# One order of wide and narrow matmuls in every unfolded unit, and eight wide matmuls that stream their columns in turn

## What is computed

```python
# first block
xn = rms_norm(x, norm_mix_g)
proj = xn @ w_in                       # 4 branches: LRU, pooling, short convolution, attention; and gates
merged = sum_k sigmoid(gate_k) * (y_k @ w_branch[k])
x = x + merged @ w_out
x = x + square(relu(rms_norm(x) @ w_mlp_up)) @ w_mlp_down        # 2048 -> 8192 -> 2048
# second block
u = rmsnorm(h, g_mix_pre)
proj = u @ w_in_2                      # dilated attention, stick-breaking attention, two gates
mix = (gate_a * (ya @ w_branch_a) + gate_b * (yb @ w_branch_b)) @ w_out_2
h = h + rmsnorm(mix, g_mix_post)
...                                    # w_up (2048 -> 2 x 5632), convolution, gelu gate, w_down,
...                                    # then a gate from w_ple_gate (2048 x 2048) on p @ w_ple_in
```

## Time and profile before

| | |
|---|---|
| time, median of 3 runs | 2932.04 us (2931.88 to 2932.59) |
| profiled execution: span from first to last instruction | 2929.8 us |
| TensorE matmul (PE) busy | 2918.4 us, 100% of the span |
| TensorE weight load (PEld) busy | 2570.8 us, 88% |
| VectorE (DVE), ScalarE (ACT), GpSimd (POOL) busy | 1920.8, 1510.8, 226.9 us |
| read from HBM | 542.25 MB, 186 GB/s over the span |
| granted TensorE clock | 1.000 |

### The profile page before, as it was taken

The page is one execution under the profiler, slowest core; times in us unless marked ns, Lnnn a source line. Parts: engine busy times, 40 slices in busy tenths (PEclk is TensorE's granted clock), DMA queues, the critical chain, the costliest instruction groups (busy, mean ns, idle before and its releaser), DMA issues. The chain is left out here.

```text
span 2929.8 us, 48840 instructions
## 1 busy us (share of the span) xinstructions
PE 2918.4 (100%) x17292; PEld 2570.8 (88%) x17292; DVE 1920.8 (66%) x2209; ACT 1510.8 (52%) x1896; POOL 226.9 (8%) x191
## 2 busy tenths in 40 slices
PE   9999999999999999999999999999999999999999
PEld 7888898998888888888888888988888888888888
DVE  6696765566665656656656566655787567757775
ACT  5576644455544444444544446555665455545564
POOL 1010020102101010000200000001000000010021
PEclk9999999999999999999999999999999999999999
DMA  8666667666565666656565555556565666666555
GB/s 248 165 186 180 173 183 229 184 177 191 194 192 182 195 191 187 193 181 197 180 197 180 167 161 168 185 185 208 159 201 180 199 187 187 192 187 187 186 158 173
DMA packets 543861, 545.94 MB, mean 186 GB/s; under 512 B 17304, under 2 KB 542112, under 8 KB 543744
## 3 DMA queue, kind: packets, MB, share of 16 engines
q1 hardware_dynamic: 540576, 536.79, 59.6%
q0 software_dynamic: 2480, 7.10, 0.9%
q10 hardware_dynamic: 688, 0.53, 0.1%
HBM read 542.25 MB, written 2.11 MB: 186 GB/s over the span
## 5 line engine op out<-in xcount | busy, mean ns | idle before, releaser
L1652 DVE TENSOR_TENSOR w_low<-raw,w_high 128x1024 fp32r<-128x1024 f32 x1012 | 1260.2, 1258 | 780.4 <-ACT w_high L1085 775.5
L1085 ACT CAST w_high<-raw 128x1024 fp32r<-128x1024 f32 x1012 | 1049.6, 1048 | 994.1 <-PE ps_gemm L704 968.9
L699 PE MATMUL ps_gemm<-act_a,w_high 128*128 128x512 f32 x4448 | 1433.5, 395 | 3.9 <-DVE act_a L2196 1.8
L699 PE MATMUL ps_gemm<-act_b,w_high 128*128 128x512 f32 x3208 | 1044.3, 395 | 0.0
L704 PEld LDWEIGHTS ps_gemm<-act_a,w_low 128*128 128x128 f32 x4608 | 861.7, 188 | 152.0
L704 PE MATMUL ps_gemm<-act_a,w_low 128*128 128x256 f32 x4608 | 991.7, 278 | 0.0
L704 PE MATMUL ps_gemm<-act_b,w_low 128*128 128x256 f32 x3520 | 778.8, 279 | 0.0
L699 PEld LDWEIGHTS ps_gemm<-act_a,w_high 128*128 128x128 f32 x4448 | 713.0, 188 | 50.4 <-issue 5.7
L704 PEld LDWEIGHTS ps_gemm<-act_b,w_low 128*128 128x128 f32 x3520 | 652.5, 189 | 96.9
L699 PEld LDWEIGHTS ps_gemm<-act_b,w_high 128*128 128x128 f32 x3208 | 524.4, 188 | 42.4
L1722 DVE TENSOR_TENSOR summ<-ps_gemm,bcopy 128x512 f32<-128x512 f32 x220 | 150.6, 685 | 8.8 <-ACT bcopy L1100 8.8
(11 more groups left out here) (291 smaller groups left out, 1204.5 us busy)
## 6 DMA issues: line engine op xcount, KB each, us to landing
raw<-in_w_in SPq DMA_DIRECT2D x348, 512.0 KB, 4.2
raw<-in_w_up SPq DMA_DIRECT2D x176, 512.0 KB, 3.5
raw<-in_w_mlp_up SPq DMA_DIRECT2D x128, 512.0 KB, 4.0
raw<-in_w_mlp_down SPq DMA_DIRECT2D x128, 512.0 KB, 3.5
raw<-in_w_down SPq DMA_DIRECT2D x88, 512.0 KB, 3.6
raw<-in_w_out SPq DMA_DIRECT2D x64, 512.0 KB, 4.7
raw<-in_w_branch SPq DMA_DIRECT2D x32, 512.0 KB, 4.0
raw<-in_w_ple_gate SPq DMA_DIRECT2D x32, 512.0 KB, 3.5
```

What stands on the lines that cost most here:

```text
L699: nc.tensor.matmul(ps[:, g, t, :], wh[:, at, o:o + P], x, start=first, stop=False, skip_group_check=True)
L1085: nc.scalar.copy(wh[:, at, :], raw[:, at, :]).then_inc(high_ready, 1)
L1652: nc.vector.tensor_tensor(wl[:, at, :], raw[:, at, :], wh[:, at, :].bitcast(F32), ALU.subtract).then_inc(split_done, 1)
```

## The change

In every unfolded unit the order within a step becomes wide, narrow, wide, narrow; folded units get the order that unfolded ones had. A table names eight phases. In these the first body is written out apart from the loop, and the very first wide matmul of the phase (first piece, k = 0, t = 0) reads and writes its 512 columns in another order: 2 (or 4) columns of the high half, the same columns of the low half, the next 2 (or 4) of the high half, and so on. Input and output follow the same order, so each column goes where it went before. There is one such matmul in each of the eight phases.

```diff
+IN_TURN = {"proj_a": 2, "gates_a2": 2, "gates_a3": 4, "gates_b1": 4, "w_out2": 2, "ffn_down0": 4, "ffn_up1": 2,
+           "ple_gate": 2}
...
-            def piece(ph, x_in, need, i, j, s, need_tile=None):
+            def piece(ph, x_in, need, i, j, s, need_tile=None, in_turn=0):
...
+                        elif k == t == 0 and in_turn:
+                            r = in_turn
+                            nc.tensor.matmul(ps[:, g, t, :].rearrange("p (e c r) -> p c e r", e=2, r=r),
+                                             wh[:, at, o:o + P], x.rearrange("p (e c r) -> p c e r", e=2, r=r),
+                                             start=first, stop=False, skip_group_check=True)
                         else:
                             nc.tensor.matmul(ps[:, g, t, :], wh[:, at, o:o + P], x,
                                              start=first, stop=False, skip_group_check=True)
...
-                    if not ph.name.startswith("mlp_"):
+                    if folded(ph, j):
                         high_product(0)
                         high_product(1)
                         low_product(0)
...
-                            piece(ph, x_in, need, i, j, s, need_tile if peeled and j == 0 else None)
+                            piece(ph, x_in, need, i, j, s, need_tile if peeled and j == 0 else None,
+                                  IN_TURN.get(ph.name, 0) if peeled and j == s == 0 else 0)
                             if once and peeled and (j, s) == at:
                                 once()
-                if once:
+                apart = once or ph.name in IN_TURN
+                if apart:
                     body(0)
-                over(pe, body, 1 if once else 0, ph.bodies)
+                over(pe, body, 1 if apart else 0, ph.bodies)
```

## The result

| | before | changed |
|---|---|---|
| time, median | 2933.43 us (7 runs, 2931.88 to 2933.58) | 2942.08 us (7 runs; six at 2937.17 to 2945.17, one at 12830.73) |
| span of the profiled execution | 2929.8 us | 2939.6 us |

The run of 12830.73 us is left out of the comparison; the other six have a median of 2941.92 us. The ratio is 1.003, 95% interval 1.002 to 1.004: about 8.5 us slower, where 7.6 us less were forecast, and outside the range. The six runs of the changed kernel are 8 us apart, those of before 2 us.

The account below looks back on a forecast made before the run. TensorE was taken to bound the kernel, by its number of matmuls times the distance between starts. Terms of -9.35 - 0.2 + 1.9 + 0 = -7.6 us took 2932.04 us to 2924.5 us, range 2922.0 to 2932.5 us.

Parts of the forecast that it names:

- What bounds the kernel: TensorE is busy 100% of the span at 2.4 GHz; time is its number of matmuls times the distance between starts.
- The order's term: Outside the mlp_ phases, all 2804 steps go from 0.69667 to 0.69333 us: -9.35 us.
- The phases that run through units. I take them quick: Phases running through units take the quick rhythm, started by eight pattern matmuls or inherited; no slow steps added there.
- called itself wrong from 280 on: Sign of failure: more than 280 of the 2804 steps slow, or a wait for `w_low` on TensorE.
- Between the small matmuls: In the two written-out stretches, a fifth of 720 steps turn slow at TensorE's restarts: +1.9 us, bounds 0 to +9.5.
- mlp_up0's start: First four pieces of mlp_up0, 16 steps, turn quick if w_out hands over the quick rhythm: -0.2 us.
- The matmuls in turn: The eight matmuls streaming columns in turn cost as much as ordinary wide ones: 0, at most 1.6 us.
- Bodies written out and buffers: Seven more phases with separate bodies on TensorE, and buffers and banks with no wait added or removed: 0.
- The order does not do it: Rival: the quick rhythm belongs to something else in the mlp_ phases, others stay as they are: 2932 us; chance 0.04.
- The rule that the prediction set beside it: Gap of N / 2.4 + 2.5 ns by columns alone: 650 ns a step in either order, the change worth nothing.
- the slow rhythm rules: Rival: slow rhythm persists after mix_* and from ffn_up0 to ffn_down2: 2947.2 us at two thirds slow, 2959.7 all; chance 0.12.

Follow-up runs that it names:

- experiment 4: Kernel before, with the order wide, wide, narrow, narrow in the mlp_ phases too and nothing of the change: 2935.62 us, ratio 1.0011.
- experiments 16 and 17: New order in chosen stretches, old-order steps as starts: first, varied counts (2944.46 us); second, one behind folded units, two behind ffn_up0's sum of squares (2927.22 us, ratio 0.998).
- experiment 16: Starts of two, three, four and one old-order steps at gates_a2, gates_a3, w_out and gates_b1, no matmul in turn: 2944.46 us, ratio 1.0042 to the kernel before.
- experiment 3: Changed kernel with the old order outside the mlp_ phases, keeping the matmuls in turn and bodies written out: 2933.29 us, ratio 1.0002.
- experiment 1: Changed kernel with an empty table: new order alone, no matmul in turn, no extra body: 2941.8 us, ratio 1.0047, runs on two levels.
- experiments 5 and 6: Changed kernel with runs of 2 in all eight phases (2938.22 us); with its table replaced by runs of 2 and 4 in mlp_ and ffn_ phases (2950.79 us).
- experiment 10: Changed kernel with single old-order steps replacing matmuls in turn, behind folded units, sums of squares and groups of small matmuls: 2929.09 us, ratio 0.9997.

## Why the prediction was wrong

- **What bounds the kernel** was right: TensorE full, no new wait, clock 1.000, the time is the distance of the starts.
- **The order's term** was right for each step (experiment 4; 88.75 against 89.17 us where it is quick) and wrong in its reach. It was taken for all 2804 steps, less a fifth of those between small matmuls.
- **"The phases that run through units. I take them quick"** is the step that failed. Its grounds were that a matmul of another pattern is a disturbance, and that the one disturbance in the trace had ended the slow rhythm. That was one case, read as a rule. A run of 4 left the slow rhythm in place (gates_a3, gates_b1, ffn_down0), a run of 2 turns the rhythm over in most states, and w_out, which had no such matmul, took the slow rhythm from the folded unit ahead of it. The prediction's own held the evidence against it: an entry into the slow rhythm with nothing irregular about it. What decides is how the last matmuls ahead stand to each other (experiments 16 and 17), and behind a folded unit they stand for slow. The changed kernel has 365 x 4 = 1460 slow steps, where the prediction called itself wrong from 280 on.
- **Sums of squares.** mlp_up0's ended the slow rhythm here as before, though not in experiment 16; slots0's and ffn_up0's started it here, for 1.2 us and 2.0 us, with ffn_down0 behind them. This was no term of the sum.
- **Between the small matmuls** a fifth was taken as slow, +1.9 us. 111 of 180 pieces were. Against the old order the two stretches lost 3.07 us, where the forecast's sum has 1.9 - 720 x 0.00333 = -0.5.
- **mlp_up0's start,** -0.2 us, did not come: w_out handed over the slow rhythm again (89.84 us in both).
- **The matmuls in turn** were taken as 0 within 0 to 1.6 us: 0.09 to 0.11 each in runs of 2, 0.01 to 0.03 in runs of 4, 0.5 us in all. The Trainium skill ("SBUF — State Buffer", "Door 1: The DMA port swizzle") is half borne out. Its SBUF lines of 16 bytes fit, as runs of 8 bytes cost and runs of 16 hardly do. That two accesses to a line are enough for full bandwidth does not fit, as a run of 2 makes two. Nor does it that any non-contiguous pattern in PSUM slows a matmul: written in runs of 8 bytes alone, it took the ordinary 0.40 us.
- **Bodies written out and buffers,** 0: right (experiment 3). The bodies are eight more than before, not seven.
- **"The order does not do it"** fell with experiment 1. The rule that the prediction set beside it was misread: the Trainium skill ("TensorE: Matmul & The Clock Gate", "Back-to-back issue gap") calls N / 2.4 + 2.5 ns the gap of an isolated matmul, and has the spacing in a stream of weight loads and matmuls set by both.
- **The rival "the slow rhythm rules"** is what happened. It was to decide from 1170 slow steps on. Here the table's 10.2 us, less 0.5 for the matmuls in turn and with the 9.35 of the order given back, make (10.2 - 0.5 + 9.35) / 0.0132 = about 1440 slow steps, against 1460 counted, 52% of 2804. Its price for a step was right, and its chance of 0.12 too small: the trace had one entry of each kind.

## What to carry to other kernels

Where one engine is full without waits, read the distances of its starts by stretch, and look for more than one rate of the same instruction order, and at the entries for the gap that goes with each; a gain that depends on such a state must be tried at each kind of entry, not summed over all steps. A rhythm seen once in a stretch that inherits it eight times is one observation, not eight. Here a step of the old order costs nothing and can be counted out so that the entry falls on the quick side; behind small matmuls the count holds only for the place where it was tried (two old steps in ffn_up0, all eleven runs), and where the stream ahead varies from run to run, the old order is the safe one.

## What the runs showed that I had not expected

- One order of matmuls, wide (512 columns) and narrow (256) in turn, runs at 0.6933 or 0.7067 us a step for hundreds of us, through loops and changes of phase. In the slow rhythm the gaps are 235, 114, 232, 118, 241, 120 ns, repeated; in the quick one 230, 117.
- Which one follows is set at the entry, by a gap of 112 ns or of 119 to 120 ns ahead of the first wide matmul, for entries out of the old order and out of folded units. All 64 such entries agree. One old step more or less, at no cost, turns it.
- A read in runs of 8 bytes turns it too, at 0.09 us, in nine entries of nine behind folded units; inside a stream it depends on the place (experiments 5 and 6). Doubling or splitting a matmul, or writing in runs of 8 bytes, did not in the one entry that each had.
- Behind small matmuls the same kernel takes one rhythm or the other from run to run, which gives levels of time 13 us apart (experiments 1 and 10). In the traces the outcome goes with the gaps ahead: of the 49 old steps behind groups of small matmuls in the written-out stretches of experiment 10, the 21 with gaps of 111 to 118 ns ahead of the new order were followed by the quick rhythm, the 15 with 120 or 121 ns by the slow one, and those with 119 ns by either (nine quick, four slow). What parts the entries at 119 ns is open; in the table of experiments 16 and 17 the four with 119 ns were all slow.
- No run of the upper level was profiled, so what differs in it is open. Why the rhythms exist at all is not shown by any run here.
